# A four-layer hybrid decoder step: conditioning units, transfer order, norm order and page latents rearranged

## The reference

```
layer 0: short gated convolution      (w_in 1024x3072, w_out 1024x1024)
layer 1: dilated window attention     (3 groups, 8 heads of 64)
layer 2: multi-scale causal pooling
layer 3: latent attention (MLA)       (8 heads; keys from 256 latent + 64 rope words)
each followed by  x += gate * (relu(h @ w1) ** 2) @ w2      (1024 -> 4096 -> 1024)
```

## Time and profile before

| | us |
|---|---|
| median of 3 runs | 2162.27 (2161.82 to 2162.92) |
| the profiled execution | 2162.28 |
| its span, first to last instruction | 2160.6 |
| TensorE busy / VectorE / ScalarE | 1966.2 / 1126.0 / 788.5 |
| mean granted TensorE clock | 0.94 |
| transfers | 399.28 MB, 185 GB/s on average |

### The profile page before, as it was taken

The page is one execution under the profiler, slowest core; times in us unless marked ns, Lnnn a source line. Parts: engine busy times, 40 slices in busy tenths (PEclk is TensorE's granted clock), DMA queues, the critical chain, the costliest instruction groups (busy, mean ns, idle before and its releaser), DMA issues.

```text
span 2160.6 us, 32785 instructions
## 1 busy us (share of the span) xinstructions
PE 1966.2 (91%) x13076; PEld 1685.6 (78%) x13076; DVE 1126.0 (52%) x1910; ACT 788.5 (36%) x1557; POOL 24.0 (1%) x44
## 2 busy tenths in 40 slices
PE   4798799999998788999969999897889999789997
PEld 1685699989996557999839999753588888679997
DVE  1552654448945346544385544577545545365532
ACT  1420443234533224432234432342344545144422
POOL 0000000000000000000000000000000000000000
PEclk9899899999997999999979999996799999799999
DMA  6764755663442796656555666521036867434442
GB/s 236 265 247 153 249 204 208 212 234 103 135 147 117 313 366 224 210 200 214 186 200 200 209 211 218 173 86 47 1 111 214 264 214 247 145 101 153 156 142 78
DMA packets 213234, 399.28 MB, mean 185 GB/s; under 512 B 7864, under 2 KB 194143, under 8 KB 196193
## 3 DMA queue, kind: packets, MB, share of 16 engines
q1 hardware_dynamic: 209552, 332.68, 44.4%
q0 software_dynamic: 2384, 60.28, 8.3%
q10 hardware_dynamic: 1161, 4.34, 0.6%
HBM read 391.23 MB, written 60.28 MB: 209 GB/s over the span
## 4 chain that ended last, share of the span: by engine, by line
PE 81%; DVE 9%; DMA 5%; ACT 2%; issue 1%; ACTq 0%; SPq 0%; POOL 0%; DVEq 0%; POOLq 0%
PE bank L1120 40%; PE bank L1026 10%; PE bank L1509 8%; PE bank L1039 5%; PE bank L1095 4%; PE bank L991 2%; PE bank L1207 2%; DVE rstd L1763 2%; DMA work<-in_keys_turned 2%; DMA work<-in_ada_w 1%; PE bank L1539 1%; PE bank L1085 1%; DMA ring<-in_mlp_w 1%; PE bank L1244 1%; DVE ring_lo L1630 1%
## 5 line engine op out<-in xcount | busy, mean ns | idle before, releaser
L1630 DVE TENSOR_TENSOR ring_lo<-ring,ring_hi 128x1024 fp32r<-128x1024 f32 (+1 forms) x324 | 380.2, 1214 | 367.8 <-ACT ring_hi L672 367.7
L672 ACT ACTIVATE ring_hi<-ring 128x1024 fp32r<-128x1024 f32 (+1 forms) x324 | 323.1, 1046 | 333.9 <-PE bank L1120 279.6
L1120 PE MATMUL bank<-hidden_hi,ring_hi 128*128 128x320 f32 x1024 | 318.9, 311 | 0.0
L1120 PE MATMUL bank<-hidden_hi,ring_lo 128*128 128x320 f32 x1024 | 316.4, 309 | 0.0
L1120 PE MATMUL bank<-hidden_lo,ring_hi 128*128 128x320 f32 x1024 | 316.3, 309 | 0.0
L1120 PE MATMUL bank<-h_hi,ring_hi 128*128 128x320 f32 x896 | 279.6, 312 | 0.1
L1120 PE MATMUL bank<-h_lo,ring_hi 128*128 128x320 f32 x896 | 276.2, 308 | 0.0
L1120 PE MATMUL bank<-h_hi,ring_lo 128*128 128x320 f32 x896 | 275.9, 308 | 0.0
L1120 PEld LDWEIGHTS bank<-hidden_hi,ring_hi 128*128 128x128 f32 x1024 | 192.2, 188 | 20.1 <-issue 20.1
L1120 PEld LDWEIGHTS bank<-hidden_lo,ring_hi 128*128 128x128 f32 x1024 | 192.3, 188 | 0.0
L1120 PEld LDWEIGHTS bank<-hidden_hi,ring_lo 128*128 128x128 f32 x1024 | 192.2, 188 | 0.0
(11 more groups left out here) (279 smaller groups left out, 3273.7 us busy)
## 6 DMA issues: line engine op xcount, KB each, us to landing
ring<-in_mlp_w SPq DMA_DIRECT2D x128, 1024.0 KB, 5.4
work<-in_ada_w SPq DMA_DIRECT2D x88, 1024.0 KB, 7.5
ring<-in_swa_w_qkv SPq DMA_DIRECT2D x18, 1024.0 KB, 5.1
out_swa_old<-in_state_swa POOLq DMA_DIRECT2D x8, 2016.0 KB, 9.6
ring<-in_conv_w_in SPq DMA_DIRECT2D x12, 1024.0 KB, 6.8
work<-in_keys_turned SPq DMA_DIRECT2D x8, 1280.0 KB, 12.8
work<-in_cache_mla SPq DMA_DIRECT2D x64, 160.0 KB, 2.2
ring<-in_ada_w SPq DMA_DIRECT2D x8, 1024.0 KB, 12.0
```

Of the source, the lines that this page charges most:

```text
L672: act.activation(ring_hi[:, place, part], ring[:, s, part], ACT.Copy).then_inc(sem("weights_hi"), 1)
L1120: mm = pe.matmul(bank[a % 4][:, 0:T], w[:, k, :], x(k), start=first and k == 0 and j == 0, stop=last and k == KD - 1 and j == 2)
L1630: dve.tensor_tensor(ring_lo[:, s, part], ring[:, s, part], ring_hi[:, place, part], ALU.subtract)\
```

## The change

- **Start.** The tables' first columns (identity, ones, eps) are loaded alone and early; the small vectors of the first norms (4 transfers) follow; convolution state, 12 small vector groups, the other tables, page table and masks are issued behind the exponential of c. Of layer 0's first conditioning part 4 blocks go to the ring and 4 to side slots (the first three without waiting, the fourth behind conv_in's first load). TensorE turns two blocks of x, then alternates the 4 units with 4 blocks of x, then the last two, vectors, three side units, the norm's sum, the late vectors, the fourth side unit. Only conv_in's first unit runs in k order (`first=1`).
- **Conditioning units.** `GAP_SIDES` is 3; in an MLP 18 units stand behind the even units 0 to 30 and units 7 and 23. Behind conv_out's units stand 2, 1, 1 and 0 side units.
- **Order of loads.** Behind the convolution the MLP's weights come first, with the side blocks between them; the last blocks of a layer are loaded one unit earlier in the next phase.
- **Norm.** ACT takes the root ahead of the second half conversion. On DVE the low part of a block follows its prompt step; the samples' low part is made in two pieces; the low weights of the second half come behind block 4.
- **MLA.** The host hands over pages as latents turned (`pages_turned`), rope words turned (`pages_rope`) and rows (`pages_rows`), and the key expansion turned. `page_turn` is gone; ACT and DVE split from SBUF; splits have 4 buffers. SP issues 3 transfers per page. New latents go out turned, and only the samples' are turned to rows (2 turns). The 16 turns of the key expansion are gone.

```diff
-GAP_SIDES = 4
+GAP_SIDES = 3
+SIDE_BEHIND = sorted([*range(0, 32, 2), 7, 23])
...
+            for v in range(SIDE):
+                load_first(v)
...
                 for u in range(16):
                     load(b1 + u, (b1 + u) % RING, KD, 256, w1[:, :, u * 256:(u + 1) * 256])
+                    if l == 0 and u < 3:
+                        for v in (((0, 15),), ((1, 0), (1, 1)), ((1, 2),))[u]:
+                            load_side(*v)
...
-            load_side(0, 15)
             mlp(0)
...
+            for n in range(NS):
+                if n == 1:
+                    sp.wait_ge(sem("mla_prompt_done"), 1)
+                if n >= 2:
+                    sp.wait_ge(sem("md_latents_split"), PAGES * (n - 1))
+                    sp.wait_ge(sem("md_keys"), PAGES * (n - 1) + 1)
+                turned_pages(n)
+                if n >= 2:
+                    sp.wait_ge(sem("md_pv"), n - 1)
+                page_rows(n)
...
             def page_hi(n, j):
-                act.wait_ge(sem("md_turned"), PAGES * n + j + 1)
-                ins = act.activation(lT_parts[0][:, :, j, :], bank[6][:, 0:2 * P].rearrange("p (c k) -> p c k", c=2), ACT.Copy)
+                if k >= 4:
+                    act.wait_ge(sem("md_keys"), k - 2)
+                act.activation(lT_parts[0][:, :, k % 4, :], md_lT[half][:, j, :, :], ACT.Copy).then_inc(sem("md_latents"), 1)
...
+            turn_x(0)
+            turn_x(1)
+            pe.wait_ge(sem("silu_ready"), 1)
+            for k in range(ADA_MAIN):
+                weights(k)
+                modulation(0, k, ring[:, k % RING, :]).then_inc(sem("unit_done"), 1)
+                turn_x(2 + k)
...
+            for v in range(SIDE):
+                first_side(v)
             pe.wait_ge(sem("x_copied"), KD)
             norm(0, split=True)
+            pe.wait_ge(sem("conv_state_landed"), 16)
+            pe.wait_ge(sem("late_vecs_landed"), 16 * LATE_VEC_DMAS)
...
-                side_unit(0, 12 + u)
+                for x in ((12, 13), (14,), (15,), ())[u]:
+                    side_unit(0, x)
...
                 sample(slice(0, 2))
+                prompt(0)
+                prompt(1)
+                if split:
+                    low(0)
+                    low_sample(slice(0, 2)).then_inc(sem("h_split"), 1)
+                sample(slice(2, KD))
+                if split:
+                    low(1).then_inc(sem("h_split"), 1)
+                for k in range(2, KD):
                     prompt(k)
+                    if split:
+                        if k == 2:
+                            dve.wait_ge(sem("h_hi"), KD * split_norm(ni) + 3)
+                            low_sample(slice(2, KD))
+                        low(k).then_inc(sem("h_split"), 1)
+                    if second and k == 4:
+                        weights_lo(second, 1, words=first_words(second, 1), halves=(1,))
```

More of the change, by code:

```diff
@@ L39 @@
 LAT = LORA + ROPE
-PG = 1 + LAT
+PG = 1 + LORA
 AB = 6 * NOPE
@@ L476, in _ @@
                 load(U, U % RING, KD, 256, conv_in[:, :, u * 256:(u + 1) * 256])
+                if u == 0:
+                    for v in range(SIDE, SIDE_FIRST):
+                        load_first(v)
                 if u == RING - 1:
@@ L766, in mlp @@
                 last_squares(2 * l + 1, w)
-                norm(2 * l + 1, split=True)
+                norm(2 * l + 1, split=True, second=w)
                 if l == 0:
@@ L815, in _ @@
             last_squares(2, "swa_qk")
-            norm(2, split=True)
+            norm(2, split=True, second="swa_qk")
             rms("swa_norm", "swa_qk", qk_chunks, qk_items, sw_sq, after=lambda u: weights_hi("swa_qk", u + 2))
@@ L863, in _ @@
             last_squares(6, "mla_qa")
-            norm(6, split=True)
+            norm(6, split=True, second="mla_qa")
             act.wait_ge(sem("side_done"), side_no(DEPTH, 0))
@@ L1165, in _, with first_side, after_conv_in @@
                 mm.then_inc(sem("x_turned"), 1)
-            pe.wait_ge(sem("start_read"), 2)
+            pe.wait_ge(sem("x_landed"), 32)
+            turn_x(0)
+            turn_x(1)
+            pe.wait_ge(sem("silu_ready"), 1)
+            for k in range(ADA_MAIN):
+                weights(k)
+                modulation(0, k, ring[:, k % RING, :]).then_inc(sem("unit_done"), 1)
+                turn_x(2 + k)
+            turn_x(KD - 2)
+            turn_x(KD - 1)
+            pe.wait_ge(sem("vecs_landed"), 16 * VEC_DMAS)
+            for t in range(2):
+                mm = turn(bank[6][:, t * P:(t + 1) * P], vec_in[:, t, :], P)
+            mm.then_inc(sem("start_turned"), 1)
+            def first_side(v):
+                pe.wait_ge(sem(f"side_landed{v % SIDE}"), 16 * (v // SIDE + 1))
+                modulation(0, ADA_MAIN + v, side[:, v % SIDE, :]).then_inc(sem("side_done"), 1)
+            for v in range(SIDE):
+                first_side(v)
             pe.wait_ge(sem("x_copied"), KD)
             norm(0, split=True)
-            pe.wait_ge(sem("silu_ready"), 1)
+            pe.wait_ge(sem("conv_state_landed"), 16)
+            pe.wait_ge(sem("late_vecs_landed"), 16 * LATE_VEC_DMAS)
+            pe.wait_ge(sem("start_read"), 1)
             for k in range(KD):
-                weights(k)
-                modulation(0, k, ring[:, k % RING, :]).then_inc(sem("unit_done"), 1)
-            pairs("conv_in", 12, KD, ni=0, each=lambda u: side_unit(0, u))
+                mm = turn(bank[6][:, 2 * P + k * 16:2 * P + (k + 1) * 16], cv_in[0:2 * NS, k * P:(k + 1) * P], 2 * NS)
+            turn(bank[6][:, 3 * P:3 * P + 64], vec_in[0:64, 2, :], 64).then_inc(sem("start_turned"), 1)
+            for v in range(SIDE, SIDE_FIRST):
+                first_side(v)
+            def after_conv_in(u):
+                if u == 0:
+                    pe.wait_ge(sem("start_read"), 2)
+                side_unit(0, u)
+            pairs("conv_in", 12, KD, ni=0, each=after_conv_in, first=1)
+            pe.wait_ge(sem("tables_landed"), 32)
             pe.wait_ge(sem("conv_mixed"), KD)
@@ L1541, in page_values @@
                     if b == 1:
-                        pe.matmul(own[:, AT_VALUES], new, ml_tok[0:TS, 2, 0:LORA], start=False, stop=False)
+                        pe.matmul(own[:, AT_VALUES], new, ml_tok[0:TS, 0:LORA], start=False, stop=False)
                         pe.matmul(own[:, 0:1], new, ones[0:TS, 0:1], start=False, stop=False)
```

287 lines of the change are left out of this document (135 added, 152 removed).

## The result

| | before | after |
|---|---|---|
| median, us | 2162.43 (4 runs) | 2126.38 (2116.81 to 2128.93, 4 runs) |
| ratio, 95% interval | | 0.9825 [0.9809, 0.9842] |
| profiled execution, span | 2162.28, 2160.6 | 2127.36, 2125.8 |
| page loop, first product to last | 1574.3 to 1845.9: 271.6 | 1543.7 to 1813.7: 270.0 |

A forecast was written before the change was run, and what follows sets the result against it. TensorE, busy 1966.2 of 2160.6 us, was taken as the bound, through needless work and standstills. Gains 25.5 + 12.5 + 4.7 - 5.9 + 3.3 + 35.5 = 75.6 us gave 2086.7 us, range 2070 to 2103.

The forecast's parts named there:

- start: Start of the kernel: first product at 40 us, third unit at 61 instead of 86.54, gain 25.5 us, bounds 17 to 29.
- behind the convolution: Step from convolution to MLP: first MLP units end at 236.7 instead of 249.27, gain 12.5 us, bounds 8 to 14.
- other gaps, units, preparation: Remaining normalisation gaps gain 4.7 us, conditioning units moved into three MLPs lose 5.9, MLA preparation gains 3.3.
- page loop: Page loop: removed turns save 33 us over 32 pairs, earlier first products 2.5; gain 35.5 us, bounds 18 to 40.
- Rival 1: SyncE's queue in the page loop: page transfers become the bound, 57 us a sequence, about 2304 us in all; chance 0.03.
- the 39 us from which, as it said, the sign turns: Page loop: slow page transfers turn the gain into a loss from 39 us per sequence, 1.6 us per issue.
- the eighth block: Start: the last conditioning block lands at 33 to 36 us, taken as 35, and its unit takes 1 us.
- The price of the new norm order: Norms: high and low part of a block follow each other directly, 1.43 us per block, where VectorE used to overlap them.
- Rival 2: Start: late small vectors land only at 42 us, first product at 48, gain 17.5, 2095 us in all; chance 0.14.
- The estimate of 33 us: Start: thirteen small loads issued into the weight stream wait 2.5 us each by the packet rule, 33 us.
- the second gap: Second normalisation gap: two units in k order take 16.7 us, ending at 503.7 instead of 505.9, gain 2.2 us.
- The range: Whole kernel: rivals 2 to 5 and the bounds fill 2070 to 2103 us; rival 1 and combinations outside, some 0.15.

The follow-up runs named there:

- one lookup: Changed kernel, SyncE looks up each page number once instead of twice, row transfers reusing the numbers read for the turned transfers: 2091.37 us, ratio 0.9665.
- without the roll: Changed kernel with GpSimd's DRAM-to-DRAM copies of the old window states removed, their outputs left unwritten: 2092.82 us, ratio 0.9678.
- the start half alone: Kernel before with all of the change but the page part: 2134.99 us, ratio 0.988.
- The six kernels named above: Changed kernel and variants (one lookup, roll removed, more lookups, roll half a sequence later, roll in small pieces); page loop entered between 1539.9 and 1545.0.

## Why the prediction was wrong

The measured leads, step by step:

| term | forecast | measured |
|---|---|---|
| start | 25.5 | 20.1 |
| behind the convolution | 12.5 | 12.2 |
| other gaps, units, preparation | 2.1 | -1.7 (+2.1 with one lookup) |
| page loop | 35.5 | 1.6 (35.0 without the roll or with one lookup) |
| behind the page loop | 0 | 2.6 |
| sum | 75.6 | 34.8 (71.1 with one lookup, by the medians) |

**The step that failed** is the page loop's "SyncE issues 24 transfers per sequence instead of 8, each with a page number at most: eight took 8.64 us, so 26 us of about 30". The undisturbed sum is even shorter, 22.5 us: the term was mis-sized, 35 us where 26 were forecast, because held-up issues stood at nothing in it. What the step left out is the roll. It stands in the trace of before, on GpSimd and in the 0.73 of the transfer engines; the forecast added up only shares and bytes ("becomes about 0.9, with a sequence of lead"), and 0.9 was right: 0.93 to 0.95 in kernels whose TensorE never waits. But beside a portion the issues themselves are held up: 12.5 us per sequence, over the bound of 29.8 by 5. Rows 12 held the trace of it, one issue of 2383 ns (732 ns is the longest without the roll).

**Rival 1 was the mechanism**, at a chance of 0.03. Its price was wrong: 2.38 us for each of 24 issues, 57 us a sequence. Measured were 35 us, short of the 39 us from which, as it said, the sign turns. It weighed "all issues slow" against "none"; the case between was missing. Removing turns from TensorE shortened the loop's period from 34.4 to 29.8 us and so brought this limit into reach, while the same change tripled the number of issues.

**Start**, 5.4 short. The first product came at 45.4, not 40. Two causes are shown. The norm's sums stood behind the third side block (landed at 31.46), and reciprocal and the first low weights (2.36 us at 38.68, left out of the forecast) followed: 2.0 of the 5.4 us came back with the sums ahead. The rest is the eighth block, whose unit ended at 39.2 (forecast: 36), its products at a granted clock of 0.50 taking 1.94 us instead of 1. From the first product to the third unit it took 21.1 us, forecast 20.9 (whose own terms, 11.5 + 7.24 + 2 x 0.99, make 20.7). The price of the new norm order, 1.43 us a block, was right, and avoidable.

**Rival 2 did not occur.** Timeline of TensorE in the changed kernel; the nine turns of the convolution state and the late vectors follow the sums without a wait, at 35.76:

```profile
34.55 1.27 PE L1113 MATMUL bank<-work,tab 128*128 128x320 f32 x2
35.76 1.32 PE L1034 MATMUL bank<-tab,work 16*128 16x16 f32 x9
37.26 1.94 PE L1138 MATMUL bank<-work,silu_c 128*32 128x512 f32 x8 [0.18 <-DMA work<-in_ada_w]
```

The last of them was issued at 15.3 and had landed by 35.76, while the transfer engines stayed full until 50. The estimate of 33 us that I had worked out from the packet rule of the Trainium skill (DMA: Bandwidth & Descriptors, Queues, rings and completion order) is refuted by this row; the rule itself isn't tested by it.

**Behind the convolution** 12.2 of 12.5; the second gap took 16.7 us in k order, as forecast, and the MLP of layer 0 grew by 2.4 us for two units (forecast 2.0). The preparation took 174.2 us from its first units to the page loop, in the kernel with the start half alone 178.8: 4.6, inside its bounds. The -1.7 comes from the window attention (320.8 us from gap to gap, 317.2 in the kernel with one lookup, whose code is the same there); the traces don't say why. The six kernels named above differ by up to 5 us at the entry of the page loop, so -1.7 and +2.1 are both within what goes unexplained there.

**The range**, 2070 to 2103, missed 2126. It took the loop's bounds from what TensorE gains (18 to 40), with no bound for a queue that is nearly full.

## What to carry to other kernels

Before an engine's chain is shortened, add up per period what every issuing queue needs, and put into that sum what others in the same period hold it up by, not only the usual duration of an issue. A large background copy counted twice here: as bytes and as held-up issues; the second didn't show while the period was 34.4 us. And where a queue is just over its period, a small saving on it (here eight lookups, 4 us) can give back the whole loop.

## What the runs showed of the hardware

- An issue on SyncE's queue isn't always 0.35 us: it took up to 10.9 us with one portion of a GpSimd DRAM-to-DRAM copy (6.75 MB) under way, and 82.79 us with four of them. With only eight transfers issued within 8.6 us beside a portion, none took over 0.72 us. Page transfers of the changed kernel land after up to 22.7 us, without the roll after 2 in the median.
- The size of the other queue's pieces matters. With pieces of one 4 KB row instead of 42 KB on average (54 MB in 1280 packets) the longest issue of the changed kernel was 2.3 us instead of 10.9, yet SyncE was still held up by 8 us in a sequence; and a page of the kernel before landed after 8.7 instead of 18.3 us. The Trainium skill (DMA: Bandwidth & Descriptors, Queues, rings and completion order) says that an engine serves its queues in turn, by packets. That agrees with the direction; it doesn't account for the 9 to 11 us that stay.
- A lookup of a page number costs SyncE 0.54 us, (8.2 - 3.85) / 8, more than issuing a row transfer (0.34 us).
- A granted clock of 0.50 (1.2 GHz) came with 12 us of standstill inside a loop that had run at 1.00.
